# Attention values as weights, probabilities as the moving operand, and the division made on the probabilities

## The reference

```python
def memory_cross_attention(q, mem_kv):      # 4 heads of 64, 256 memory rows, once in each of two layers
    ...
    scores = jnp.einsum('bshd,bmhd->bhsm', q, k).astype(jnp.float32) * (XA_HEAD_DIM ** -0.5)
    p = jax.nn.softmax(scores, -1).astype(v.dtype)
    o = jnp.einsum('bhsm,bmhd->bshd', p, v)
    return o.reshape(b, s, D_XA)

def chunk_causal_attention(q, k, v):        # 8 heads, values of 64; blocks of 128 queries
    ...
        s = jnp.einsum('bqhd,bkhd->bhqk', qi, k, preferred_element_type=jnp.float32) * scale
        ...
        mask = key_chunk[None, :] <= q_chunk[:, None]
        pr = jax.nn.softmax(jnp.where(mask, s, -jnp.inf), axis=-1).astype(v.dtype)
        return jnp.einsum('bhqk,bkhd->bqhd', pr, v)
```

## Time and profile before

| | |
|---|---|
| runs shown, median | 1559.37 us (1559.23 to 1559.47, 3 runs) |
| the profiled execution | 1558.53 us, of which the span is 1556.8 us |
| TensorE busy | 1524.9 us, 98% |
| VectorE, ScalarE, GpSimd busy | 1127.5, 887.3, 54.8 us |
| granted TensorE clock, mean | 0.994 of full |

### The profile page before, as it was taken

One profiled execution on the slowest core, in us unless ns is written; L12 is line 12 of the kernel. 1 busy time (PEld: TensorE's weight loads), 2 busy tenths in 40 slices (PEclk: granted clock), 3 DMA queues, 4 the chain that ended last, 5 costly groups with the idle time before them and its releaser, 6 DMA issues.

```text
span 1556.8 us, 21695 instructions
## 1 busy us (share of the span) xinstructions
PE 1524.9 (98%) x8798; PEld 1338.1 (86%) x8798; DVE 1127.5 (72%) x1624; ACT 887.3 (57%) x1355; POOL 54.8 (4%) x87
## 2 busy tenths in 40 slices
PE   8999999999999999999999999799999999999996
PEld 7888899888889888889988888699999888788885
DVE  7566665666657665666686566778887879989997
ACT  6555463555554554457456455455556667777774
POOL 0000000000000000000210000100001110100000
PEclk9999999999999999999999999999999999999999
DMA  8755454555545555444357544355433769899993
GB/s 346 266 189 191 161 194 160 215 217 190 200 179 180 212 190 202 154 155 143 129 193 263 214 167 179 104 193 190 163 136 135 279 240 377 328 353 349 360 365 113
DMA packets 49049, 333.71 MB, mean 214 GB/s; under 512 B 5808, under 2 KB 5936, under 8 KB 10544
## 3 DMA queue, kind: packets, MB, share of 16 engines
q1 hardware_dynamic: 47216, 321.39, 56.1%
q10 hardware_dynamic: 1728, 10.88, 1.8%
HBM read 331.20 MB, written 1.05 MB: 213 GB/s over the span
## 4 chain that ended last, share of the span: by engine, by line
PE 93%; DVE 4%; ACT 1%; POOL 1%; issue 0%; DMA 0%; SPq 0%; DVEq 0%
PE psw L516 60%; PE psy L516 31%; PE psw L519 2%; DVE wlo L1789 2%; DVE x L1885 0%; POOL r L2564 0%; DVE x L1872 0%; POOL rstd L2522 0%; DVE xs L1798 0%; ACT xs L1223 0%; DMA raw<-in_ws 0%; DVE r L1854 0%; DVE r L1885 0%; DVE r L2473 0%; DVE ar L2043 0%
## 5 line engine op out<-in xcount | busy, mean ns | idle before, releaser
L1789 DVE TENSOR_TENSOR wlo<-raw,whi 128x1024 fp32r<-128x1024 f32 (+2 forms) x552 | 639.0, 1205 | 104.5 <-ACT whi L1223 99.5
L516 PE MATMUL psw<-xs,whi 128*128 128x512 f32 (+2 forms) x2416 | 658.4, 346 | 6.8 <-DVE wlo L1789 6.8
L1223 ACT ACTIVATE whi<-raw 128x1024 fp32r<-128x1024 f32 (+2 forms) x552 | 535.5, 1031 | 11.7 <-PE psy L516 6.8
L516 PE MATMUL psw<-xs,wlo 128*128 128x256 f32 (+1 forms) x1864 | 494.0, 281 | 0.0
L516 PEld LDWEIGHTS psw<-xs,whi 128*128 128x128 f32 (+1 forms) x2416 | 406.9, 188 | 55.3 <-DVE wlo L1789 6.8
L516 PEld LDWEIGHTS psw<-xs,wlo 128*128 128x128 f32 (+1 forms) x1864 | 351.7, 189 | 15.8
L516 PE MATMUL psw<-whi,xs 128*128 128x512 f32 (+1 forms) x736 | 189.1, 365 | 2.5 <-DVE wlo L1789 1.6
L516 PE MATMUL psy<-whi,hhi 128*128 128x512 f32 x472 | 157.9, 390 | 0.0
L516 PE MATMUL psy<-whi,hlo 128*128 128x512 f32 x472 | 157.8, 389 | 0.0
L516 PE MATMUL psy<-wlo,hhi 128*128 128x512 f32 x472 | 157.7, 389 | 0.0
L516 PEld LDWEIGHTS psw<-whi,xs 128*128 128x128 f32 x736 | 131.7, 189 | 24.6 <-DVE wlo L1789 2.3
(11 more groups left out here) (299 smaller groups left out, 1511.4 us busy)
## 6 DMA issues: line engine op xcount, KB each, us to landing
raw<-in_ws SPq DMA_DIRECT2D x257, 1024.0 KB, 4.9
ar<-in_ws SPq DMA_DIRECT2D x32, 1024.0 KB, 7.2
gb<-in_ln ACTq DMA_DIRECT2D x8, 1024.0 KB, 5.4
raw<-in_ws SPq DMA_DIRECT2D x9, 768.0 KB, 4.3
raw<-in_ws SPq DMA_DIRECT2D x4, 672.0 KB, 4.0
raw<-in_ws SPq DMA_DIRECT2D x8, 256.0 KB, 6.2
ar<-in_memT SPq DMA_DIRECT2D x2, 1024.0 KB, 7.7
ar<-in_xT SPq DMA_DIRECT2D x4, 256.0 KB, 4.8
```

The costliest lines, as they stand in the source:

```text
L516: return e.matmul(o, l, rr, start=start, stop=stop)
L1223: return e.activation(o, i, ACT.Copy, **k)
L1789: e.tensor_tensor(wlo[i % NS][:, c0:c1], raw_t[slot[i]][:, c0:c1], whi[i % NS][:, c0:c1].bitcast(f32), ALU.subtract).then_inc(*made.up((i, ...
```

## The change

Both attentions now give the values as weights (64 columns) and the turned probabilities as the moving operand, up to 256 tokens at once. The output has features on the partitions: an even head goes to partitions 0 to 63 and the odd head beside it to 64 to 127 of the same bank, so nothing is turned after it. Since tokens are now along the free axis of the output, the division by the sums moves ahead of the turn: VectorE divides `pbuf` in the memory attention (`divide`), and in the eight-head attention VectorE takes a reciprocal for each head and ScalarE scales `S` in place by two copies (`probabilities`). The copies of the outputs into `mhi`/`mlo` stay.

```diff
-            def value(l, h):
-                o = claim(4, "mixed", l) if h == 0 else place["mixed", l]
-                p2 = mem_of[l].pT[h % 2]
-                need.wait_ge(*act.at("probT", l, h))
-                for t in range(2):
-                    for m in range(2):
-                        c = 256 * t + 64 * h
-                        ins = mm(o[:, c:c + 64], p2[:, m, 128 * t:128 * t + 128], vm[:, l, m, 64 * h:64 * h + 64], m == 0, m == 1)
-                ins.then_inc(*pe.up(("value", l, h)))
-            def finish(l):
...
+            def values(l, pair):
+                b = claim(4, "mixedT", l) if pair == 0 else place["mixedT", l]
+                need.wait_ge(*act.at("probT", l, 2 * pair + 1))
+                for m in range(2):
+                    for i in range(2):
+                        h = 2 * pair + i
+                        ins = mm(b[64 * i:64 * i + 64, 256 * pair:256 * pair + 256], vm[:, l, m, 64 * h:64 * h + 64],
+                                 mem_of[l].pT[i][:, m, :], m == 0, m == 1)
+                ins.then_inc(*pe.up(("value", l, pair), *([("bank", ("mixedT", l))] if pair else [])))
...
 # TensorE, conv_mixer (turn now waits for VectorE's "prob" instead of ScalarE's)
-                         lambda: (value(0, 0), turn(0, 1)), lambda: (value(0, 1), turn(0, 2)), lambda: (value(0, 2), turn(0, 3)),
-                         lambda: value(0, 3), lambda: finish(0), lambda: None]
+                         lambda: turn(0, 1), lambda: (values(0, 0), turn(0, 2)), lambda: turn(0, 3), lambda: values(0, 1),
+                         lambda: None, lambda: None]
 # TensorE, mlstm_mixer
+                steps = [lambda: (turn(1, 0), weights(0), weights(1)), lambda: turn(1, 1),
+                         lambda: (values(1, 0), turn(1, 2), attend(0)), lambda: (states(0), turn(1, 3)),
+                         lambda: (values(1, 1), attend(1)), lambda: states(1)]
 # TensorE, eight heads
             def turn_p(h):
-                need.wait_ge(*act.at("S", h))
+                need.wait_ge(*act.at("probabilities", h))
...
+            def values_of(h):
+                q, pair = h // 4, h // 2
+                if h % 2 == 0:
+                    return
+                b = place["headsT", q] if pair % 2 else claim(4 + q, "headsT", q)
+                need.wait_ge(*act.at("pT", h))
+                c = 256 * (pair % 2)
+                for i in range(2):
+                    mm(b[64 * i:64 * i + 64, c:c + 256], va_s[:, 0, h - 1 + i, :], pTb[i][:, 0:256], True, False)
+                for i in range(2):
+                    ins = mm(b[64 * i:64 * i + 64, c + 128:c + 256], va_s[:, 1, h - 1 + i, :], pTb[i][:, 256:384], False, True)
...
-            for q in range(2):
-                b = bank("headsT", q)
-                need.wait_ge(*dve.at("empty", ("heads", 1)))
...
 # ScalarE, eight heads
+            def probabilities(h):
+                need.wait_ge(*dve.at("ri", h))
+                for t, (c0, c1) in enumerate(halves):
+                    ins = copy(S[h % 3][:, c0:c1], S[h % 3][:, c0:c1], scale=ri_s[:, 2 * h + t:2 * h + t + 1])
+                ins.then_inc(*act.up(("probabilities", h)))
-                for back, stage in ((3, turn_p), (0, turn_qk), (1, scores)):
+                for back, stage in ((2, probabilities), (3, turn_p), (0, turn_qk), (1, scores)):
 # VectorE, memory attention
+            def divide(l, *heads):
+                m = mem_of[l]
+                for h in heads:
+                    need.wait_ge(*act.at("prob", l, h))
+                    then(e.reciprocal(m.ri[:, 2 * h:2 * h + 2], m.sm[:, 2 * h:2 * h + 2]))
+                    for t in range(2):
+                        ins = e.tensor_scalar(m.pbuf[:, h, t, :], m.pbuf[:, h, t, :], m.ri[:, 2 * h + t:2 * h + t + 1], None, ALU.mult)
+                    ins.then_inc(*dve.up(("prob", l, h)))
-                         lambda: None, lambda: scale(0), lambda: finish(0), lambda: None]
+                steps = [lambda: (score(0, 0), score(0, 1)), lambda: (score(0, 2), score(0, 3), divide(0, 0, 1)), lambda: divide(0, 2, 3),
+                         lambda: None, lambda: None, lambda: None, lambda: None, lambda: finish(0), lambda: None]
...
+                w.rows(4, {0: decays, 1: lambda: (score(1, 0), score(1, 1)), 2: lambda: (decay_columns(), score(1, 2), divide(1, 0, 1)),
+                           3: lambda: (score(1, 3), divide(1, 2))})
+                steps = [lambda: divide(1, 3), lambda: None, lambda: attend(0), lambda: states(0), lambda: attend(1),
 # VectorE, eight heads
             for step in range(12):
+                if 0 <= step - 2 < 8:
+                    h = step - 2
+                    need.wait_ge(*act.at("S", h))
+                    e.reciprocal(ri_s[:, 2 * h:2 * h + 2], sm_s[:, 2 * h:2 * h + 2]).then_inc(*dve.up(("ri", h)))
                 if 0 <= step - 1 < 8:
                     scores(step - 1)
...
-            then(e.reciprocal(ri_s, sm_s))
-            need.wait_ge(*pe.at("values", 7))
-            for t in range(2):
...
```

More of the change, by code:

```diff
@@ L744, in turn @@
                 b = bank("probT", l, h)
-                need.wait_ge(*act.at("prob", l, h))
+                need.wait_ge(*dve.at("prob", l, h))
                 for m in range(2):
@@ L998, in turn_p @@
                 ins.then_inc(*pe.up(("bank", ("pT", h))))
[L1000 to L1005, removed]
-                need.wait_ge(*act.at("pT", h))
-                mm(o[0][:, 64 * h:64 * h + 64], p[:, 0:128], va_s[:, 0, h, :], True, True)
-                mm(o[1][:, 64 * h:64 * h + 64], p[:, 128:256], va_s[:, 0, h, :], True, False)
-                mm(o[1][:, 64 * h:64 * h + 64], p[:, 256:384], va_s[:, 1, h, :], False, True).then_inc(*pe.up(("values", h)))
+            def values_of(h):
[3 more added lines that the diff above has]
+                b = place["headsT", q] if pair % 2 else claim(4 + q, "headsT", q)
+                need.wait_ge(*act.at("pT", h))
+                c = 256 * (pair % 2)
[3 more added lines that the diff above has]
+                    ins = mm(b[64 * i:64 * i + 64, c + 128:c + 256], va_s[:, 1, h - 1 + i, :], pTb[i][:, 256:384], False, True)
+                ins.then_inc(*pe.up(("values", pair), *([("bank", ("headsT", q))] if pair % 2 else [])))
             for step in range(12):
-                for back, stage in ((4, values), (3, turn_p), (1, scores), (0, turn_qk)):
+                for back, stage in ((4, values_of), (3, turn_p), (1, scores), (0, turn_qk)):
                     if 0 <= step - back < 8:
@@ L1335, in turn @@
                 if h > 1:
-                    need.wait_ge(*pe.at("value", l, h - 2))
+                    need.wait_ge(*pe.at("value", l, h // 2 - 1))
                 from_bank(("probT", l, h), mem_of[l].pT[h % 2].rearrange("p m n -> p (m n)"), flat, ("probT", l, h))
@@ L1599, in turn_p @@
                 if h > 1:
-                    need.wait_ge(*pe.at("values", h - 2))
+                    need.wait_ge(*pe.at("values", h // 2 - 1))
                 from_bank(("pT", h), pTb[h % 2], lambda b: b[:, 0:384], ("pT", h))
+            def probabilities(h):
[3 more added lines that the diff above has]
+                ins.then_inc(*act.up(("probabilities", h)))
             for step in range(12):
-                for back, stage in ((3, turn_p), (0, turn_qk), (1, scores)):
+                for back, stage in ((2, probabilities), (3, turn_p), (0, turn_qk), (1, scores)):
                     if 0 <= step - back < 8:
@@ L2248, in vector @@
                 gate_half()
-            need.wait_ge(*act.at("S", 7))
-            then(e.reciprocal(ri_s, sm_s))
-            need.wait_ge(*pe.at("values", 7))
[L2252 to L2256, removed]
             gate_half()
```

14 lines of the change are left out of this document (removed).

## The result

The changed kernel takes 1563.88 us (median of 15 runs, 1561.87 to 1564.42) against 1559.06 (15 runs, 1558.58 to 1560.50): ratio 1.0027, 95% interval 1.0020 to 1.0034. It is slower by 0.3%. The prediction was 1555.4, faster by 0.25%.

The account below looks back on a forecast made before the run. TensorE, busy 98% of the span, was taken to bound the kernel. Gains of 1.70 (layer 0), 1.26 (layer 1) and 1.04 (eight heads) made 4.0 us: 1554.5 us profiled, 1555.4 median, range 1553.4 to 1561.4.

Parts of the forecast that it names:

- Layer 1: 3.36 - 2.10 = 1.26: Second memory attention: four value blocks (3.36 us) removed, two pairs of heads (2.10) put in, 1.26 us gained.
- the removed closing turn: Layer 1's last turn, 0.44 us: counted as no gain, since TensorE would only wait longer for the silu.
- the four rivals: Column halves run serially (0.20); full drains at each switch (0.15); larger division waits (0.13); no waits and free switches (0.07).
- The pair of heads: TensorE's new value block for two heads: 1.05 us in a memory layer, 0.84 in the eight-head attention.
- The overlap: Two heads' matmuls run side by side on separate column halves: 0.85 us per memory pair instead of 1.71.
- The switch: Going into the new array shape and back: 0.20 us per pair block, with 0 and 0.43 as ends.
- Layer 0: First memory attention: 3.80 us removed from TensorE, 2.10 put in, 1.70 us gained.
- The silu wait: End of the second mixer: TensorE's wait for ScalarE's silu grows from 0.30 to about 0.7 us.
- The division on VectorE: Memory layers: 0.8 us of added VectorE work per head, costed at nothing because TensorE would not wait for it.
- The eight heads: Eight-head attention: 0.16 us gained in the steps and 0.88 from closing turns, 1.04 us in all.
- The waits: Start of the eight-head attention: TensorE waits for the division, 0.8 then 0.5 us, 1.36 us in all.
- The sum: Whole kernel: 1.70 + 1.26 + 1.04 = 4.0 us gained, giving 1554.5 us profiled, 1555.4 as a median.

Follow-up runs that it names:

- E2: The kernel before, with only layer 1's turned output put in bank 5 instead of the next rotating bank: 1566.51 us, ratio 1.0044.
- E1: The changed kernel with `finish(1)` one step earlier on both copying engines, ahead of the taps and `states(1)`: 1555.77 us, ratio 0.9978 to before.
- E7: E1 with each head's two matmuls together and, in layer 0, both heads on array columns 0 to 63: 1558.54 us, ratio 0.9991 to before.
- E5: The kernel before with only the memory part of the change, and `finish(1)` one step earlier: 1556.97 us, ratio 0.9983.
- E3: The kernel before with only the eight-head part of the change: 1559.01 us, ratio 0.9997.
- E6: The changed kernel with layer 1's output in bank 7, claimed by "o" with its first tile's second half: 1560.76 us, ratio 1.0009 to before.

## Why the prediction was wrong

**The step that failed** is the one for layer 1. "Layer 1: 3.36 - 2.10 = 1.26" took the removed closing turn only as a longer wait for the silu. It listed what the closing turn cost and not what it did besides: it moved the output out of bank 4, the bank of the next projection, into one that nobody wanted, and so uncoupled `finish` from TensorE. With the turn gone, two copies whose place had cost nothing stood between TensorE and its next bank. The text asked of each added operation what is queued behind it, and of no bank who holds it, until when, and who claims it next. None of the four rivals has this mechanism, and the range ended at 1561.4. E2 shows the cause without the rest of the change, E1 shows the change without the cause.
The Trainium skill, "Perfetto Trace Analysis", "Matmuls", says to rotate independent groups through the banks so that the copy out of one overlaps the matmuls of the next. The kernel before did that at this place and the changed one doesn't: 5.27 us of wait.

**What the bank costs.** Against E1, 5.6 us until "o" starts and 2.4 more from there to the piece behind its first tile (7.09 us from start to start against 4.71, in which E1 has its silu wait): with what little comes back behind it 7.8. About 0.5 of this is a gain of the early finish itself. In the kernel before, ScalarE's copy to `mhi` (0.49 us in the chain, at 764.03) stands ahead of the silu for which TensorE waits, and in E1 it doesn't. That leaves 7.4 for the bank, and it closes the sum of layer 1: 4 x 0.84 - (1.01 + 0.15 + 1.01) = 1.2 gained, less 7.4, is the measured loss of 6.2. The trace of before could have told the wait: there too VectorE's copy into `mlo` ends 6.2 us behind that tile (759.31 to 765.49; in the changed kernel 757.67 to 763.87), and TensorE has only 0.7 us of other work in between. The 3.1 behind it stood in none of the rows that I had read.

**The pair of heads.** Predicted 0.85 + 0.20 = 1.05 us in the memory layers and 0.84 in the eight-head attention. Measured 1.01 and 0.80, with 0.15 more on the turn directly behind. The overlap, on which most of the predicted gain hung, is there in full (E7). The switch costs 0.15 within the block and 0.15 on a turn behind it, against 0.43 for a score block.
The Trainium skill, "TensorEngine Tiling (Array Packing)", Key Properties, speaks of a drain for a change of the mode without telling kinds apart; the trace shows less for this shape, 0.15 to 0.30, than for the row shape's 0.43.

**Layer 0.** Predicted 1.70, measured 1.46: 3.80 - (1.01 + 0.15 + 1.01) = 1.63, less 0.2 in the two tiles behind the second pair (11.70 us against 2 x 5.75).

**Layer 1 without the bank.** Predicted 1.26, measured 1.23 (E5), and that is luck. Up to the start of "o" E5 is 1.66 us ahead of the kernel before and keeps that until 1000 us, because with the early finish the closing turn is a gain too: 3.80 - 2.17 = 1.63. The silu wait in E1 is 0.25 us, not the 0.7 that I had expected of a kernel without the turn. Then E5 loses 0.45 at the stretch of low clock behind the wait at 1000 us, which nothing in the change touches. The division on VectorE cost nothing in either layer, as predicted.

**The eight heads.** Predicted 1.04, measured 0.29 (changed kernel) and 0.28 (E3). Removed in the steps: 8 x 0.61 = 4.88; put in their place 4 x 0.80 = 3.20, three slower turns of 0.15, and waits of 1.6. That is a loss of 0.4, where I had a gain of 0.16; the closing turns gave their 0.88. The two make 0.5, and 0.2 of loss spread over the steps isn't placed. The waits came at the predicted place and only there, with 1.26 us in the rows against 1.36 predicted, but they cost 1.55.

**The sum.** Without the bank, 1.46 + 1.23 + 0.29 = 2.98 us, where 4.0 was predicted: 1556.4 rather than 1555.4. With the bank 4.5 are lost instead, and 1.04 us of spread ahead of the first changed instruction in the profiled execution: span 1556.8 + 4.5 + 1.0 = 1562.3.

## What to carry to other kernels

When an operation is removed, ask what else it did: here a turn that cost 0.44 us also moved data out of a bank that the next stage wanted, and its absence cost about 7.4 us. For every buffer that now lives longer or elsewhere, write down its last reader, what stands ahead of that reader in its queue, and who claims the buffer next; the place of a copy is free only as long as nobody waits for its source. And a wait of TensorE of some microseconds has a second price, the clock behind it: here 1.6 to 3.1 us for waits of 3.2 to 5.3, and none for one of 1.6. When differences of a microsecond matter, compare the traces stage by stage, because stretches of low clock come and go between executions in places that the change doesn't touch.

## What the runs showed that I had not expected

**The clock after a wait.** It is full (2.4 GHz) at first and falls to 1.2 GHz before the wait ends: in E2's window from 763 to 765 us it stands at 0.52 on average, and TensorE does nothing there. Then the first matmuls behind the wait run at 1.2 GHz. Three waits at this place: 3.19 us cost 1.6 (E6), 4.83 cost 2.4 (E2, where the chain has 6.60 for the 24 matmuls), 5.27 cost 3.1 (the changed kernel). That is about half of the wait in each, but it is no rule. The wait of 4.92 us at 1000 us is alike in all traces, and the stretch of layer 1 behind it takes 107.7 to 109.0 us, longer where the clock stays low for longer. And a wait of 1.61 us at 1360 us leaves the clock at 1.00 in all eleven traces; here in the kernel before:

```profile
1361.91 0.72 PE L516 MATMUL psw<-whi,xs 128*128 128x512 f32 x2 [1.61 <-DVE wlo L1789]
```
```profile
1361.90:1366.00 4.10, 4.09 (x18) 3.38 (x19) 4.10 (x5) 3.31 (x4) 0.00 (x0) 1.00 0.77 262
```

The Trainium skill, "TensorE: Matmul & The Clock Gate", "HAM oscillation — how this bites in real kernels", describes this double price for a kernel that waits for transfers. The traces here agree that the wait is paid for twice, with a wait for a bank.

**The clock without a wait.** At 719 us it falls to 1.2 GHz for about 3 us, with TensorE busy for the whole of the three windows shown above, behind a block of eight records of 1.99 us that uses 4 rows of the array where a projection uses 128 (`4*128` in the timeline against `128*128`). Six of the eleven traces have it and five don't. It costs 1.5 us, as much as the terms that this change was about, and the runs of one version often lie in two groups so far apart. What tips it is open: the kernel before and E2 have the same instructions up to there, and so have E1 and E5, and in both cases one trace has the dip and the other hasn't.

**Column halves.** Two heads on separate columns run together although both read all 128 rows, in either order of issue: 1.01 and 1.02 us against 1.87 on the same columns.
